# An unused buffer of 32 bytes ahead of the activation buffers of a two-block transformer kernel

## The chip, the cores and the metric

The kernel runs on one core of one Trainium2 chip. The metric is the device time in microseconds of one execution. TensorE (PE in the profile) multiplies, VectorE (DVE) and ScalarE (ACT) do the elementwise work, and SyncE (SP) issues the DMAs. SBUF, the on-chip memory, has 128 partitions; a buffer takes the same range of bytes in each of them, and "address" below means the byte in a partition where it starts.

## The reference

The reference runs 256 tokens of width 1024 through two blocks of two layers each, batch 1, float32.

```
def first_block(...):                                   # two layers
    h = rms_norm(x, norm_mix_g[l]); z = h @ w_in[l]
    y_rg = rg_lru(...) * gelu(a_y)                      # gated recurrence
    y_ml = mlstm_branch(...)                            # chunked matrix memory
    y_xa = memory_attention(xa_q, mem_n, w_kv[l])
    merged = g0 * (y_rg @ w_br_rg) + g1 * (y_ml @ w_br_ml) + g2 * (y_xa @ w_br_xa)
    x = x + merged @ w_out[l]
    x = x + (swiglu(h2, w1, w3, w2) if l == 0 else moe_swiglu(h2, ...))   # 8 experts, top 2
def second_block(...):                                  # two layers, tokens and 256 context tokens
    h_x = modulate(rmsnorm(x, ...), shift, scale)       # shift and scale from silu(c) @ ada_w
    o_x, o_c = mixer_ab(...) if layer == 0 else mixer_c(...)
    x = x + mod_x[2] * o_x; x = x + mod_x[5] * swiglu_2(h_x, w1, w3, w2)   # layer 0: ctx as well
```

All weights together are some 700 MB, and each is used once, on at most 512 tokens.

## The kernel before

**Precision and the general product.** Weights arrive in float32 as tiles of 128 x 2048 (1 MB; 8 blocks of 128 inputs by 256 outputs, for the experts' second product 2 blocks by 1024). A tile lands in RAW (three slots), in the expert stage in turn in RAW or in one of five of the F buffers. ACT copies it to WH in the format float32r (line 1899), and DVE subtracts that from the tile and writes the rest to WL (line 2299). Activations are kept as such pairs too: PH and PL (three pairs of 8 x 256), HPH and HPL (8 x 512), HDH and HDL (8 x 512), and YS with the experts' results. Each product is then three matmuls in float32r, in this order (lines 1566 to 1568):

```
T_.matmul(out, lh, rh, start=first, stop=False)
T_.matmul(out, lh, rl, start=False, stop=False)
last = T_.matmul(out, ll, rh, start=False, stop=end)
```

The second argument is the stationary operand (up to 128 columns are loaded into the array), the third the moving one (256 or 512 columns are streamed). In the trace a matmul is named PS<-moving,stationary.

**Forms.** In the rows form (most dense layers: the input projections, the branches, both feed-forward networks) the stationary operand is a slice of 128 columns of WH or WL, and the moving one a block of activations with 256 or 512 tokens. In the token form (values of the attentions, `tok` and `dtok`) it is the other way round: 128 tokens are stationary and 256 columns of WH or WL stream. The experts' first products (lines 1517 to 1519: stationary the gathered tokens in PH, PL or YS, moving WH or WL, 256 columns) and second products (lines 1835 to 1837: 512 columns of WH or WL against PH or PL) are like the token form. Line 1806 gathers an expert's tokens and lines 1846 and 1847 scatter its result back; both of their operands are activation buffers. Line 1699 to 1701 multiply the recurrence's gate weights, a tile with 36 columns.

**Order.** A planner writes one list of units by its own costs; each engine's program runs through that list. Engines wait for one another by semaphores. A tile's DMA waits until the tile that had the slot is split, WH and WL (three slots each) until the product that used them is done. The core runs first the first block (0 to some 1183 us its dense and attention parts, to some 2157 us the experts) and then the second.

**Placement.** `build` allocates the buffers one after another in one stack. Each takes its size, rounded up to a multiple of 32 bytes. `with ExitStack() as s1` opens a group whose buffers are freed at its end, so that the next ones lie over them: CAU, TMP1, F and P of the first block share their bytes with HP, BIAS, CST2, BAND, GN, TMP2, G, PQ and HD of the second, and YS (behind PAD) with F0 and F1. The last buffer ahead of all these is MOD.

Of the kernel before, what the change touches and what calls it, by code (L numbers as in the profile page):

```python
# [2919 lines left out]
def build(nc, io):  # L2920
    with ExitStack() as ctx:
        def sb(name, shape, dt=F32, stack=ctx):
            return stack.enter_context(nc.sbuf_tensor(name, shape, dt))
        mem = {}
        mem["RAW"] = sb("RAW", [128, NRAW, 2048])
        mem["WH"] = sb("WH", [128, NHL, 2048], F32R)
        mem["WL"] = sb("WL", [128, NHL, 2048], F32R)
        mem["X"] = sb("X", [128, 8, T])
        mem["CTX"] = sb("CTX", [128, 8, T])
        mem["PAR"] = sb("PAR", [128, NPAR])  # L2930
        mem["CST"] = sb("CST", [128, NCST])
        mem["SM"] = sb("SM", [128, 128])
        mem["RT"], mem["MK"], mem["GT"] = (mem["SM"][:, a:b] for a, b in ((0, 66), (66, 82), (82, 98)))
        mem["IDX"] = mem["SM"][:, 98:114].bitcast(U32)
        mem["LAMS"] = sb("LAMS", [128, 16])
        mem["ACOL"] = sb("ACOL", [128, 8])
        mem["R"] = sb("R", [128, 3, T])
        mem["LV"] = sb("LV", [128, 2])
        mem["LVS"] = sb("LVS", [128, 8])
        mem["POS"] = sb("POS", [128, 32])  # L2940
        mem["GC"] = sb("GC", [128, 3])
        mem["FLAG"] = sb("FLAG", [1, 1], mybir.dt.int32)
        mem["C32"] = sb("C32", [128, 262])
        mem["MROW"] = sb("MROW", [128, 512])
        mem["MOD"] = sb("MOD", [128, 2, 2, 48])
        mem["PS"] = ctx.enter_context(nc.psum_tensor("PS", [128, 8, 512], F32))
        with ExitStack() as s1:
            mem["CAU"] = sb("CAU", [128, 384], F32, s1)
            mem["TMP1"] = sb("TMP1", [128, 4, T], F32, s1)
            mem["F"] = [mem["CTX"] if i == 4 else sb(f"F{i}", [128, 8, T], F32, s1) for i in range(8)]  # L2950
            mem["P"] = [(sb(f"PH{i}", [128, 8, T], F32R, s1), sb(f"PL{i}", [128, 8, T], F32R, s1)) for i in range(3)]
        with ExitStack() as s2:
            sb("PAD", [128, 384 + 4 * T], F32, s2)
            mem["YS"] = sb("YS", [128, 16, T], F32R, s2)
        mem["HP"] = (sb("HPH", [128, 8, 512], F32R), sb("HPL", [128, 8, 512], F32R))
        mem["BIAS"] = sb("BIAS", [128, 512])
        mem["CST2"] = sb("CST2", [128, NCST2])
        mem["BAND"] = sb("BAND", [128, 640], F32R)
        mem["GN"] = sb("GN", [128, 2, 2, 2, 8])
        mem["TMP2"] = sb("TMP2", [128, 4, 512])  # L2960
        with ExitStack() as s3:
            mem["G"] = [sb(f"G{i}", [128, 4, 512], F32, s3)[:, :, :] for i in range(6)]
            mem["PQ"] = sb("PQ", [128, 3584], F32, s3)
            mem["LM"], mem["LAMB"] = mem["PQ"][:, 0:128], mem["PQ"][:, 128:384]
        with ExitStack() as s4:
            mem["HD"] = (sb("HDH", [128, 8, 512], F32R, s4), sb("HDL", [128, 8, 512], F32R, s4))
        v = views(mem)
        plan = Plan(io, mem, v)
        ledger = Ledger(lambda name: ctx.enter_context(nc.semaphore(name)))
        none = Nothing()  # L2970
        tensor_program(none, none, Engine(ledger, none, "pe", True), plan, mem, v)
        scalar_program(none, none, Engine(ledger, none, "act", True), plan, mem, v)
        vector_program(none, none, Engine(ledger, none, "dve", True), plan, mem, v)
        sync_program(none, none, Engine(ledger, none, "sp", True), plan, mem, v)
        block = ctx.enter_context(nc.Block())

        @block.sync
        def _(eng):
            sync_program(nc, nc.sync, Engine(ledger, eng, "sp", False), plan, mem, v)

        @block.tensor
        def _(eng):
            tensor_program(nc, nc.tensor, Engine(ledger, eng, "pe", False), plan, mem, v)

        @block.scalar
        def _(eng):
            scalar_program(nc, nc.scalar, Engine(ledger, eng, "act", False), plan, mem, v)

        @block.vector
        def _(eng):  # L2990
            vector_program(nc, nc.vector, Engine(ledger, eng, "dve", False), plan, mem, v)
# [104 lines left out]
```

How the kernel before makes its waits and increments, by code:

```python
    def wait_ge(self, what, *key):  # L90
        what = self.pre + what
        if self.counting:
            return
        n = self.ledger.value[(what,) + key]
        if self.seen.get(what, 0) < n:
            self.eng.wait_ge(self.ledger.sem(what), n)
            self.seen[what] = n
# [5 lines left out]
    def freed(self, key):  # L103
        if key is None or self.counting:
            return
        by = self.ledger.handed.get((self.pre,) + key)
        if by is not None:
            return self.wait_for(by)
        for what in ("free_a", "free_d"):
            if (self.pre + what,) + key in self.ledger.value:
                return self.wait_ge(what, *key)
        raise KeyError(key)
# [1 line left out]
    def wait_for(self, thing):  # L115
        n = self.ledger.value[thing]
        if self.seen.get(thing[0], 0) < n:
            self.eng.wait_ge(self.ledger.sem(thing[0]), n)
            self.seen[thing[0]] = n
# [1 line left out]
    def turn(self, made):  # L121
        made.then_inc(*self.done("turn_" + self.tag, self.steps))
        self.wait_ge("turn_" + self.tag, self.steps)
        self.steps += 1
# [1396 lines left out]
    def weight(key):  # L1522
        t = plan.tile[key]
        pe.wait_ge("w_hi", t.s)
        pe.wait_ge("w_lo", t.s)
        return t
# [1 line left out]
    def consts():  # L1528
        pe.wait_ge("par")
        pe.wait_ge("cst")
# [1 line left out]
    def lin(name, t, i, part, parts, side=None):  # L1532
# [27 lines left out]
        for j, (lh, ll, rh, rl) in enumerate(pairs):  # L1560
            if norm:
                pe.wait_ge("lo", norm, ks[j] // 2)
            if "each" in g.more:
```

## Time and profile before

| what | value |
|---|---|
| time, median of 3 runs | 3374.03 us (3371.98 to 3382.2) |
| span of the profiled execution | 3378.7 us |
| PE, weight loads, DVE, ACT busy | 96%, 88%, 69%, 54% |
| mean granted clock of TensorE | 0.976 |
| moved by DMA | 723.62 MB, mean 214 GB/s |

The profiled span is taken on the core from the first to the last instruction. Busy time of PE is the time in which at least one matmul is under way. Matmuls overlap (the next one starts while the last results of the one ahead drain), so PE's pace is read from the distance between starts in the timeline, and not from the length of one.

### The profile page before, as it was taken

What the parts mean: (1) busy time and instruction counts of PE and PEld (TensorE: products, weight loads), DVE (VectorE), ACT (ScalarE), POOL (GpSimd) and SP (SyncE); (2) the same over time, 40 slices, a digit from 0 to 9 for tenths busy, and PEclk for the clock granted to TensorE, in tenths of its full rate; (3) what the DMA queues carried; (4) which work ended last, traced back from release to release, by engine and by line L of the source; (5) the groups of instructions that cost most, each with busy time, mean ns of one, the idle gap of its engine ahead of it and who ended that gap; (6) DMA issues with size and microseconds to landing.
All of it is one profiled execution on the core that took longest, in us unless ns stands there. A gap on an engine that the chain in (4) does not pass through costs nothing.

```text
span 3378.7 us, 56020 instructions
## 1 busy us (share of the span) xinstructions
PE 3229.4 (96%) x24147; PEld 2988.9 (88%) x24147; DVE 2334.0 (69%) x2984; ACT 1831.6 (54%) x2188; POOL 0.2 (0%) x4
## 2 busy tenths in 40 slices
PE   8999999999899899999999999899899999999898
PEld 7998999999889799999999999778687989985698
DVE  6877655577776688888888888755575565556455
ACT  5564544455644477777777777633454444334443
POOL 0000000000000000000000000000000000000000
PEclk9999999999999899999999999999899999998899
DMA  6433565454335699899899899621333466530353
GB/s 255 164 138 125 187 236 193 158 193 159 125 125 188 269 367 363 331 357 357 331 356 356 338 357 354 249 85 63 113 136 127 141 234 251 199 124 13 145 187 118
DMA packets 102812, 723.62 MB, mean 214 GB/s; under 512 B 11424, under 2 KB 13344, under 8 KB 16672
## 3 DMA queue, kind: packets, MB, share of 16 engines
q1 hardware_dynamic: 102560, 719.97, 57.3%
q8 instruction: 194, 3.18, 0.4%
q14 instruction: 58, 0.48, 0.0%
HBM read 718.87 MB, written 1.05 MB: 213 GB/s over the span
## 4 chain that ended last, share of the span: by engine, by line
PE 80%; DVE 10%; ACT 7%; issue 2%; DMA 1%; SPq 0%; DVEq 0%; ACTq 0%
PE PS L1566 14%; PE PS L1568 13%; PE PS L1567 13%; PE PS L1517 6%; PE PS L1519 6%; PE PS L1518 6%; DVE WL L2299 4%; PE PS L1835 3%; PE PS L1836 3%; PE PS L1837 3%; ACT WH L1899 3%; PE PS L1677 2%; PE PS L1648 2%; PE PS L1621 1%; PE PS L1665 1%
## 5 line engine op out<-in xcount | busy, mean ns | idle before, releaser
L2299 DVE TENSOR_TENSOR WL<-RAW,WH 128x2048 fp32r<-128x2048 f32 (+2 forms) x428 | 962.8, 2252 | 548.3 <-ACT WH L1899 543.2
L1899 ACT ACTIVATE WH<-RAW 128x2048 fp32r<-128x2048 f32 (+2 forms) x428 | 803.4, 1880 | 243.1 <-PE PS L1568 182.6
L1566 PE MATMUL PS<-PH,WH 128*128 128x256 f32 x2464 | 705.5, 286 | 22.6 <-ACT F L1981 6.1
L1567 PE MATMUL PS<-PL,WH 128*128 128x256 f32 x2464 | 696.4, 283 | 0.0
L1568 PE MATMUL PS<-PH,WL 128*128 128x256 f32 x2464 | 696.3, 283 | 0.0
L2299 DVE TENSOR_TENSOR WL<-F,WH 128x2048 fp32r<-128x2048 f32 x210 | 480.8, 2290 | 79.8 <-ACT WH L1899 79.1
L1566 PE MATMUL PS<-HPH,WH 128*128 128x256 f32 (+1 forms) x1648 | 493.2, 299 | 17.8 <-ACT WH L1899 8.7
L1566 PEld LDWEIGHTS PS<-PH,WH 128*128 128x128 f32 x2464 | 468.9, 190 | 29.2 <-issue 20.5
L1567 PE MATMUL PS<-HPL,WH 128*128 128x256 f32 (+1 forms) x1648 | 481.2, 292 | 0.0
L1568 PE MATMUL PS<-HPH,WL 128*128 128x256 f32 (+1 forms) x1648 | 480.6, 292 | 0.0
L1567 PEld LDWEIGHTS PS<-PL,WH 128*128 128x128 f32 x2464 | 469.1, 190 | 0.6
L1568 PEld LDWEIGHTS PS<-PH,WL 128*128 128x128 f32 x2464 | 468.7, 190 | 0.0
L1899 ACT ACTIVATE WH<-F 128x2048 fp32r<-128x2048 f32 x210 | 403.7, 1923 | 72.1 <-PE PS L1837 48.2
L1517 PE MATMUL PS<-WH,PH 128*128 128x256 f32 x1456 | 417.4, 287 | 2.0 <-DVE WL L2299 1.1
L1518 PE MATMUL PS<-WL,PH 128*128 128x256 f32 x1456 | 407.4, 280 | 0.0
L1519 PE MATMUL PS<-WH,PL 128*128 128x256 f32 x1344 | 376.9, 280 | 0.0
L1566 PEld LDWEIGHTS PS<-HPH,WH 128*128 128x128 f32 x1648 | 317.7, 193 | 36.4 <-issue 20.3
L1567 PEld LDWEIGHTS PS<-HPL,WH 128*128 128x128 f32 x1648 | 318.1, 193 | 4.3
L1568 PEld LDWEIGHTS PS<-HPH,WL 128*128 128x128 f32 x1648 | 317.7, 193 | 4.5
L1517 PEld LDWEIGHTS PS<-WH,PH 128*128 128x128 f32 x1456 | 275.2, 189 | 5.4 <-ACT WH L1899 1.2
L1518 PEld LDWEIGHTS PS<-WL,PH 128*128 128x128 f32 x1456 | 275.6, 189 | 2.8
L1519 PEld LDWEIGHTS PS<-WH,PL 128*128 128x128 f32 x1344 | 253.9, 189 | 0.0
(394 smaller groups left out, 4972.1 us busy)
## 6 DMA issues: line engine op xcount, KB each, us to landing
F<-in_moe_w SPq DMA_DIRECT2D x210, 1024.0 KB, 5.6
RAW<-in_ffn_w SPq DMA_DIRECT2D x130, 1024.0 KB, 5.0
RAW<-in_moe_w SPq DMA_DIRECT2D x126, 1024.0 KB, 5.2
RAW<-in_w_in SPq DMA_DIRECT2D x64, 1024.0 KB, 5.0
F<-in_ada_w SPq DMA_DIRECT2D x18, 1024.0 KB, 11.3
RAW<-in_w_kv SPq DMA_DIRECT2D x16, 1024.0 KB, 5.0
G<-in_ada_w SPq DMA_DIRECT2D x15, 1024.0 KB, 9.0
RAW<-in_w_in_ab SPq DMA_DIRECT2D x12, 1024.0 KB, 5.0
```

Of the source, the lines that this page charges most:

```text
L1517: T_.matmul(out, lh, rh, start=i == 0, stop=False)
L1518: T_.matmul(out, lh, rl, start=False, stop=False)
L1519: last = T_.matmul(out, ll, rh, start=False, stop=i == n - 1)
L1566: T_.matmul(out, lh, rh, start=first, stop=False)
L1567: T_.matmul(out, lh, rl, start=False, stop=False)
L1568: last = T_.matmul(out, ll, rh, start=False, stop=end)
L1648: last = T_.matmul(ps, l, r, start=i == 0, stop=i == len(ops) - 1 and not spec["bias"])
L1835: T_.matmul(out, oh[:, c], wh, start=j == 0 and k == 0, stop=False)
L1836: T_.matmul(out, oh[:, c], wl, start=False, stop=False)
L1837: last = T_.matmul(out, ol[:, c], wh, start=False, stop=j == 13 and k == 1)
L1899: S.activation(mem["WH"][:, t.s % NHL, 0:m], v.raws[t.slot][:, 0:m], ACT.Copy).then_inc(*ac.done("w_hi", t.s))
L2299: V.tensor_tensor(mem["WL"][:, t.s % NHL, 0:m], v.raws[t.slot][:, 0:m], mem["WH"][:, t.s % NHL, 0:m].bitcast(F32), sub).then_inc(*dv.done( ...
```

## The change

One line is added to `build`, behind the last of the buffers that live through the whole kernel. It allocates a buffer EDGE of 8 float32 values (32 bytes) in each partition, which nothing reads or writes.

```
--- before.py
+++ after.py
@@ -2944,6 +2944,7 @@
         mem["MROW"] = sb("MROW", [128, 512])
         mem["MOD"] = sb("MOD", [128, 2, 2, 48])
         mem["PS"] = ctx.enter_context(nc.psum_tensor("PS", [128, 8, 512], F32))
+        sb("EDGE", [128, 8])
         with ExitStack() as s1:
             mem["CAU"] = sb("CAU", [128, 384], F32, s1)
             mem["TMP1"] = sb("TMP1", [128, 4, T], F32, s1)
```

The instructions, their order, their waits and the DMAs are the same on every engine. What moves is the address of every buffer that is allocated behind EDGE, by 32 bytes (addresses of the built programs):

| buffer | address before | modulo 64 | address after | modulo 64 |
|---|---|---|---|---|
| RAW, WH, WL | 16512, 41088, 65664 | 0 | the same | 0 |
| X, CTX | 90240, 98432 | 0 | the same | 0 |
| MOD | 116320 | 32 | the same | 32 |
| CAU and HPH | 117088 | 32 | 117120 | 0 |
| F0 and YS | 122720 | 32 | 122752 | 0 |
| HPL | 133472 | 32 | 133504 | 0 |
| TMP2 | 157280 | 32 | 157312 | 0 |
| G0 and HDH | 165472 | 32 | 165504 | 0 |
| PH0, PL0 | 180064, 188256 | 32 | 180096, 188288 | 0 |
| PQ | 214624 | 32 | 214656 | 0 |

The buffers between them (F1 to F7, PH1 to PL2, G1 to G5, HDL, BIAS, CST2, BAND, GN, TMP1) are 32 modulo 64 before and 0 after in the same way. Rows inside the buffers are multiples of 512 or 1024 bytes apart, so the blocks that the products read start like their buffer; after the change they have the same address modulo 128 as the blocks of WH and WL. Small buffers that stay where they are (SM, LAMS, ACOL, LVS, MROW, MOD) keep their 32 modulo 64.

## Rows read from the trace of the kernel before

**Rows 1.** The page: span, busy time of each engine, granted clock in 40 slices.
```profile
span 3378.7 us, 56020 instructions
...
PE 3229.4 (96%) x24147; PEld 2988.9 (88%) x24147; DVE 2334.0 (69%) x2984; ACT 1831.6 (54%) x2188; POOL 0.2 (0%) x4
```

**Rows 2.** Stretches: us, then busy us of PE, PEld, DVE, ACT, POOL; clock, DMA share.
```profile
124.50:146.00 21.50, 21.50 (x187) 21.50 (x186) 20.78 (x21) 7.69 (x5) 0.00 (x0) 1.00 0.53 192
340.00:680.00 340.00, 336.11 (x2865) 332.24 (x2864) 195.87 (x229) 155.74 (x168) 0.00 (x0) 1.00 0.54 195
1183.00:2157.00 974.00, 973.77 (x6963) 910.03 (x6962) 841.40 (x609) 705.16 (x612) 0.00 (x0) 1.00 0.93 349
```

**Rows 3.** The page's chain that ended last, by engine and by line.
```profile
PE 80%; DVE 10%; ACT 7%; issue 2%; DMA 1%; SPq 0%; DVEq 0%; ACTq 0%
PE PS L1566 14%; PE PS L1568 13%; PE PS L1567 13%; PE PS L1517 6%; PE PS L1519 6%; PE PS L1518 6%; DVE WL L2299 4%; PE PS L1835 3%; PE PS L1836 3%; PE PS L1837 3%; ACT WH L1899 3%; PE PS L1677 2%; PE PS L1648 2%; PE PS L1621 1%; PE PS L1665 1%
```

**Rows 4.** PE's groups by shape: label moving,stationary; busy us, mean ns, idle before.
```profile
L1566 PE MATMUL PS<-PH,WH 128*128 128x256 f32 x2464 | 705.5, 286 | 22.6 <-ACT F L1981 6.1 <-DVE PL L2390 5.6 <-issue 4.3
...
L1566 PE MATMUL PS<-HPH,WH 128*128 128x256 f32 x1552 | 452.3, 291 | 13.5 <-DVE HPL L2393 7.2 <-ACT WH L1899 4.3 <-ACT G L2053 0.8
...
L1517 PE MATMUL PS<-WH,PH 128*128 128x256 f32 x1456 | 417.4, 287 | 2.0 <-DVE WL L2299 1.1 <-ACT PL L2172 1.0
...
L1566 PE MATMUL PS<-HDH,WH 128*128 128x256 f32 x352 | 99.2, 282 | 0.0
...
L1566 PE MATMUL PS<-WH,PH 128*128 128x256 f32 x160 | 44.7, 279 | 0.0
...
L1566 PE MATMUL PS<-HPH,WH 128*128 128x512 f32 x96 | 40.9, 426 | 4.4 <-ACT WH L1899 4.4
```

**Rows 5.** PE in order of time, feed-forward: first and last of 195 matmuls.
```profile
519.84 0.28 PE L1566 MATMUL PS<-PH,WH 128*128 128x256 f32 x1
...
542.79 0.28 PE L1568 MATMUL PS<-PH,WL 128*128 128x256 f32 x1
```

**Rows 6.** PE in order of time, token form of the keys and values: 192 matmuls.
```profile
124.05 0.28 PE L1566 MATMUL PS<-WH,PH 128*128 128x256 f32 x1
...
146.33 0.28 PE L1568 MATMUL PS<-WH,PL 128*128 128x256 f32 x1
```

**Rows 7.** PE in order of time, 512 columns, projection stage: 23 matmuls.
```profile
2299.17 0.39 PE L1567 MATMUL PS<-HPL,WH 128*128 128x512 f32 x1
...
2304.30 0.40 PE L1568 MATMUL PS<-HPH,WL 128*128 128x512 f32 x1
```

**Rows 8.** PE in order of time, 512 columns, an expert's second product: 12 matmuls.
```profile
1356.49 0.39 PE L1835 MATMUL PS<-WH,PH 128*128 128x512 f32 x1
...
1359.05 0.40 PE L1837 MATMUL PS<-WH,PL 128*128 128x512 f32 x1
```

**Rows 9.** PE in order of time, an expert's scatter back: 16 matmuls.
```profile
1305.58 0.28 PE L1846 MATMUL PS<-PL,YS 128*128 128x256 f32 x1
...
1307.37 0.28 PE L1847 MATMUL PS<-PL,YS 128*128 128x256 f32 x1
```

**Rows 10.** PE in order of time, gate weights of 36 columns: 24 matmuls.
```profile
169.16 0.28 PE L1699 MATMUL PS<-PH,WH 128*36 128x256 f32 x1
...
169.85 0.28 PE L1699 MATMUL PS<-PH,WH 128*36 128x256 f32 x1
...
171.86 0.28 PE L1701 MATMUL PS<-PH,WL 128*36 128x256 f32 x1
```

**Rows 11.** Splits of a weight tile, by source: ACT's copy and DVE's subtraction.
```profile
L1899 ACT ACTIVATE WH<-RAW 128x2048 fp32r<-128x2048 f32 x409 | 780.3, 1911 | 214.9 <-PE PS L1568 154.5 <-PE PS L1837 29.6 <-PE PS L1519 14.3
...
L1899 ACT ACTIVATE WH<-F 128x2048 fp32r<-128x2048 f32 x210 | 403.7, 1923 | 72.1 <-PE PS L1837 48.2 <-PE PS L1519 23.9
```

**Rows 12.** The page's DMA issues: KB each, median us from issue to landing.
```profile
F<-in_moe_w SPq DMA_DIRECT2D x210, 1024.0 KB, 5.6
...
RAW<-in_moe_w SPq DMA_DIRECT2D x126, 1024.0 KB, 5.2
```

More of the change, by code:

```diff
@@ L2946, in build @@
         mem["PS"] = ctx.enter_context(nc.psum_tensor("PS", [128, 8, 512], F32))
+        sb("EDGE", [128, 8])
         with ExitStack() as s1:
```

## The prediction

> **What bounds the kernel now.** I read the page's busy times first. TensorE (PE) is busy 3229.4 of 3378.7 us, DVE 2334.0 and ACT 1831.6 [rows 1]. The stretches show where that holds: in the feed-forward stage from 340 to 680 us PE is busy 336.1 of 340 us, and in the expert stage from 1183 to 2157 us 973.8 of 974 us [rows 2]. So nearly everywhere the time is the number of matmuls times the step from one matmul's start to the next one's. The mean length of a matmul in the groups (280 to 290 ns) is not that step, since matmuls overlap; the step has to be read from the timeline. The chain that ended last agrees: PE has 80% of it, and lines 1566, 1567 and 1568 (the general product) 40% of the span [rows 3].
>
> The change moves no instruction. It moves the start of every buffer behind it by 32 bytes, so the question is which engine's work depends on where in 64 bytes an operand starts. The raw tiles RAW, the split tiles WH and WL, X and CTX start at multiples of 64 in both kernels. All of F, P (PH, PL), HP, HD, YS, G, PQ, TMP start at 32 past one before, and at 0 after. I call the two places 32 and 0. In the trace's names the first operand of a matmul is the moving one (it streams 256 or 512 columns), the second the stationary one (128 columns of weights). Four combinations of moving and stationary places exist, and the kernel before has three of them:
>
> Moving at 32, stationary at 0 (the rows form, activations stream against split weights): in the feed-forward stage 195 matmuls start from 519.84 to 542.79 us, 194 steps, 22.95 us, **118.3 ns** a step [rows 5].
>
> Moving at 0, stationary at 32 (the token form and the experts' up products, split weights stream against activations): 192 matmuls from 124.05 to 146.33 us, 191 steps, **116.65 ns** [rows 6]. Both stretches have the granted clock at 1.00, the 2.4 GHz level [rows 2]. It is the same line 1566 and the same 256 columns, and the groups show the same difference in the length of one: 282 ns for PS<-HDH,WH and 279 ns for PS<-WH,PH, both without any idle time before them [rows 4].
>
> Both at 32 (an expert's scatter back): 16 matmuls from 1305.58 to 1307.37 us, 15 steps, **119.3 ns** [rows 9].
>
> Both at 0 is what the change makes of all of them, and no row shows it. That is the open price here.
>
> **The change part by part.** The unused buffer itself costs no instruction. Its worth is in these parts.
>
> The rows form with 256 columns. Its groups count 2464, 1552 and 352 on each of three lines [rows 4], 13,104 matmuls; the output projection of the last attention (lines 1582 to 1584) adds 192 by the code. Bounds for its step after the change: from above 119.3 ns, the nearest row in which both operands have the same place [rows 9]; from below 115.0 ns, the lowest step of a stretch with 256 columns, the first six steps from 169.16 to 169.85 us of the product with only 36 weight columns [rows 10] (over all its 23 steps, to 171.86 us, it is 117.4). I take 116.65, because it is the row with an aligned moving operand and the same 128 weight columns [rows 6], and because 512 columns take 233.2 ns a step (22 steps from 2299.17 to 2304.30 us) with the moving operand at 32 [rows 7] and 232.7 ns (11 steps from 1356.49 to 1359.05 us) with it at 0 [rows 8], twice 116.6. A step in proportion to the columns looks like the stream's own pace, on which 118.3 stands 1.65 ns. The gain is 13,296 x 1.65 ns = 21.9 us.
>
> The scatter back and the gather of the experts, both at 32 before, 128 matmuls each by the code: 2.7 ns off each of 256, 0.7 us.
>
> The experts' up products and the token form, 3 x (1456 + 336) and 480 matmuls, only the stationary operand moves from 32 to 0: bounds 115.6 to 119.3 ns, taken as no change (116.65), by the same stream pace. The 512-column products likewise: rows 7 and 8 differ by half a nanosecond although opposite operands are at 32.
>
> Sum on PE: 22.6 us. How much reaches the end? Lines 1566 to 1568 hold some 1673 us of steps (13,104 x 118.3 ns, 480 x 116.65 ns, 288 x 233.2 ns), and the chain gives them 40% of 3378.7, 1351 us, or 81% [rows 3]; so at least 18.3 us. Where PE is busy without a gap [rows 2] all of it counts. I take 21 us. What is late next there: nothing, since in the feed-forward stage DVE is busy 195.9 and ACT 155.7 of 340 us and the DMA share is 0.54 [rows 2].
>
> ACT and DVE. ACT's split copy takes 1911 ns from RAW (at 0) and 1923 ns from F (at 32), 210 of these [rows 11]: 2.5 us of ACT time, hidden, because PE stands still 0.2 us in the whole expert stage [rows 2]. If that cover were gone it would be worth at most 2.5 us.
>
> DMA. Expert tiles that go to F land 5.6 us after issue, those to RAW 5.2 us [rows 12]. If that 0.4 us is the place of the destination it goes away, and again PE has no wait in that stage that it could shorten: nothing. That stage moves 349 GB/s at a DMA share of 0.93 [rows 2], so it could not run much faster either.
>
> The Trainium skill speaks against all this: its page "Advanced Engine Details and Errata", section Memory Cachelines, gives SBUF lines of 16 bytes, full speed for accesses that stay in one. Both 0 and 32 are starts of such a line, so by that rule the sum would be nothing, against the 22.6 us above. The trace has a step that differs by 1.65 ns between two placements [rows 5, 6], which the rule alone doesn't explain.
>
> **The profiled execution and the median.** The profiled span is 3378.7 us, the median of the three runs 3374.0 us, 4.7 us below it. A difference of 21 us is the same on either. Predicted: 3374 - 21 = 3353 us.
>
> **The rivals.**
>
> *The two costs add up.* From the three rows, the stationary place costs 119.3 - 118.3 = 1.0 ns and the moving one 119.3 - 116.65 = 2.65 ns; both at 0 would be 115.65 ns. The rows form gains 13,104 x 2.65 = 35 us, the others 5,856 x 1.0 = 6 us, scatter and gather 1 us: 42 us, 3332 us. For it: the narrow product reaches 115.0 ns [rows 10]. Against it: 512 columns take twice 116.6 ns [rows 7, 8]. With all at 115.0 ns it would be 53 us, 3321 us, the far end. A still lower step (106.7 ns is 256 columns at 2.4 GHz) has no row near it.
>
> *Slower: the operands get in each other's way when they start at the same place.* PE reads the stationary columns of the next matmul while the present one streams. The only matmuls before with both operands at one place have the longest step, 119.3 ns [rows 9]; the mixed ones have 118.3 and 116.65 [rows 5, 6]. If the cause is equal places and not the place 32, the change puts every product there: 13,104 x 1.0 + 5,856 x 2.65 = 13 + 16 = 29 us more, 3403 us. It decides from a step of 117.8 ns upward: there what the rows form wins and what the others lose cancel. Against it: in both mixed cases the distance is 32 modulo 64, yet they differ by 1.65 ns, so the moving operand's own place must count for something.
>
> *Nothing.* The 1.65 ns belongs to the form and not to the place: in the rows form the stationary operand is a slice of half a row of a split tile and the moving one a whole row of activations. Then the step stays at 118.3 ns, gain 0, 3374 us. This is also what the skill's line of 16 bytes would give. Against it: 512 columns in the rows form show no extra [rows 7].
>
> **How the numbers follow.** The forecast (3349 to 3358 us) has a chance of 0.48, adding up 0.17, nothing 0.17, equal places 0.18. A measurement of this kernel can tell about 0.3% (10 us) from no change; so faster 0.65, same 0.17, slower 0.18. The range leaves out only the slower case: from 3321 us less 3 us of spread to 3374 us plus 6 us (the runs before lie within 10 us), 3318 to 3380 us.
>
> **What would show it.** In the profile after, the feed-forward stretch that took 22.95 us for 194 steps takes 22.6 us; length of PS<-HDH,WH falls from 282 to 279 ns; the token form keeps 116.65 ns and the 512-column products 233 ns; scatter back falls from 119.3 to some 116.7 ns; the expert stage keeps its 974 us. If the scatter back keeps 119.3 ns and the expert stage grows by some 15 us, equal places are the cause. If both forms fall to 115.7 ns, the costs add up. If the rows form keeps 118.3 ns, the place is not the cause. The forecast is wrong too if a stage's time moves while its matmul step does not.

## The result and the profile after: slower by 0.7%, because moving and stationary operands now start at equal places

The changed kernel takes 3397.19 us (median of four runs, 3396.51 to 3401.66), the kernel before beside it 3373.01 us (median of four, 3367.34 to 3382.2). The ratio is 1.0069, interval 1.0054 to 1.0084: 24.2 us slower. The prediction was 3353 us, 3318 to 3380 us. Both its sign and its range were wrong; the case it had as the slower rival (3403 us, with a chance of 0.18) is the one that happened.

The page of the profiled execution after: span and busy times, the chain by engine, and the issues of the experts' tiles.

```profile
span 3394.7 us, 56020 instructions
...
PE 3254.8 (96%) x24147; PEld 3022.7 (89%) x24147; DVE 2337.2 (69%) x2984; ACT 1829.2 (54%) x2188; POOL 0.2 (0%) x4
...
PE 79%; DVE 11%; ACT 6%; issue 2%; DMA 2%; SPq 0%; DVEq 0%; ACTq 0%
...
F<-in_moe_w SPq DMA_DIRECT2D x210, 1024.0 KB, 5.6
...
RAW<-in_moe_w SPq DMA_DIRECT2D x126, 1024.0 KB, 5.4
```

PE's busy time rose by 25.4 us against [rows 1], the span by 16.0 us; all other engines kept theirs. F's tiles still land 5.6 us after issue although F now starts at a multiple of 64 [rows 12]: the destination's place was not what they lost against RAW.

The groups of PE and ACT by shape, after (busy us, mean ns of one, idle before):

```profile
L1566 PE MATMUL PS<-PH,WH 128*128 128x256 f32 x2464 | 709.5, 288 | 20.3 <-ACT F L1981 5.9 <-DVE PL L2390 4.8 <-issue 4.1
...
L1517 PE MATMUL PS<-WH,PH 128*128 128x256 f32 x1456 | 420.9, 289 | 2.1 <-ACT PL L2172 1.1 <-DVE WL L2299 1.0
...
L1566 PE MATMUL PS<-HDH,WH 128*128 128x256 f32 x352 | 99.9, 284 | 0.0
...
L1899 ACT ACTIVATE WH<-F 128x2048 fp32r<-128x2048 f32 x210 | 402.3, 1917 | 74.1 <-PE PS L1837 45.4 <-PE PS L1519 28.7
```

Each of the three PE groups grew by about 2 ns a matmul (from 286, 287 and 282 ns in [rows 4] to 288, 289 and 284), with about the same idle time ahead of them. The exact steps are in PE's timeline after. In order: the rows form in the feed-forward stage (195 matmuls, as in [rows 5]); the token form (192, as in [rows 6]); 512 columns in the projection stage (23, as in [rows 7]); an expert's second product (12, as in [rows 8], of a later expert); a scatter back (16, as in [rows 9], of a later expert).

```profile
519.68 0.28 PE L1566 MATMUL PS<-PH,WH 128*128 128x256 f32 x1
...
542.96 0.28 PE L1568 MATMUL PS<-PH,WL 128*128 128x256 f32 x1
...
124.20 0.28 PE L1566 MATMUL PS<-WH,PH 128*128 128x256 f32 x1
...
147.12 0.28 PE L1568 MATMUL PS<-WH,PL 128*128 128x256 f32 x1
...
2283.57 0.40 PE L1567 MATMUL PS<-HPL,WH 128*128 128x512 f32 x1
...
2288.60 0.39 PE L1568 MATMUL PS<-HPH,WL 128*128 128x512 f32 x1
...
2152.51 0.40 PE L1835 MATMUL PS<-WH,PH 128*128 128x512 f32 x1
...
2155.03 0.39 PE L1837 MATMUL PS<-WH,PL 128*128 128x512 f32 x1
...
1825.22 0.28 PE L1846 MATMUL PS<-PL,YS 128*128 128x256 f32 x1
...
1827.01 0.28 PE L1847 MATMUL PS<-PL,YS 128*128 128x256 f32 x1
```

Last less first, by the number of steps: 23.28 us by 194 is **120.0 ns** (before 118.3), 22.92 by 191 is **120.0 ns** (before 116.65), 5.03 by 22 is **228.6 ns** (before 233.2), 2.52 by 11 is **229.1 ns** (before 232.7), and the scatter back keeps 119.3 ns. The timeline gives times to 0.01 us, so over 15 steps a value is sure only to 0.7 ns, over 11 steps to 0.9 ns, and over 190 steps to 0.05 ns. So both forms with 256 columns now have one step, higher than either had, and the 512-column products have become faster.

What that makes over the whole kernel follows from the means of all gapless stretches of the two traces. The rows form with 256 columns has 118.32 ns before and 119.92 after, the token form 116.68 and 119.92, the experts' first product 116.92 and 119.65, 512 columns 233.20 and 229.13 with experts, 233.28 and 228.70 without. 13,296 x 1.60 + 960 x 3.24 + 5,376 x 2.73 - 1,344 x 4.07 - 288 x 4.58 is 21.3 + 3.1 + 14.7 - 5.5 - 1.3 = 32 us. Measured are 24.2 us.

The stage in which PE hardly waits (busy 1010.18 of 1015.70 us before) shows the sum best. Below are the stretches up to the first expert, the experts, and the rest, first of the kernel before, then after (columns: busy us of PE, PEld, DVE, ACT, POOL; granted clock, DMA share, GB/s):

```profile
0.00:1160.30 1160.30, 1094.40 (x8784) 1058.19 (x8784) 787.66 (x1132) 580.21 (x742) 0.20 (x4) 0.98 0.49 177
1160.30:2176.00 1015.70, 1010.18 (x7219) 943.55 (x7220) 872.24 (x634) 733.00 (x636) 0.00 (x0) 1.00 0.91 343
2176.00:3378.70 1202.70, 1124.83 (x8147) 987.18 (x8145) 674.11 (x1219) 518.38 (x812) 0.00 (x0) 0.96 0.38 141
```

```profile
0.00:1168.70 1168.70, 1110.77 (x8783) 1073.26 (x8784) 788.35 (x1132) 579.47 (x742) 0.20 (x4) 0.98 0.49 176
1168.70:2193.30 1024.60, 1019.43 (x7220) 959.68 (x7220) 873.77 (x634) 732.79 (x636) 0.00 (x0) 1.00 0.91 340
2193.30:3394.70 1201.40, 1124.57 (x8146) 989.74 (x8145) 675.05 (x1219) 516.91 (x811) 0.00 (x0) 0.97 0.39 141
```

The expert stage grew by 8.9 us, with the clock at 1.00 in both; its terms of the sum give 14.7 - 5.5 = 9.2 us. The first part grew by 8.4 us. The last part did not grow in these two executions, but its granted clock was 0.97 after and 0.96 before. Of a span of 3378.7 us at a mean of 0.976 some 160 us are at the lower level (1.2 GHz), of 3394.7 us at 0.979 some 142 us. The profiled executions therefore differ by 16.0 us while the medians differ by 24.2 us, and the comparisons below go by medians.

### The profile page after: what moved, and what is told of

Its sections match the earlier page's. It is cut to its first block, busy times and chain, and to the rows that moved or that the text cites. A ratio compares the mean times of both kernels' runs of the same rounds, so it can differ in the third digit from the quotient of the medians.

```text
span 3394.7 us, 56020 instructions
## 1 busy us (share of the span) xinstructions
PE 3254.8 (96%) x24147; PEld 3022.7 (89%) x24147; DVE 2337.2 (69%) x2984; ACT 1829.2 (54%) x2188; POOL 0.2 (0%) x4
## 4 chain that ended last, share of the span: by engine, by line
PE 79%; DVE 11%; ACT 6%; issue 2%; DMA 2%; SPq 0%; DVEq 0%; ACTq 0%
PE PS L1566 14%; PE PS L1567 13%; PE PS L1568 13%; PE PS L1517 6%; PE PS L1518 6%; PE PS L1519 6%; DVE WL L2299 4%; PE PS L1835 3%; PE PS L1836 3%; PE PS L1837 3%; ACT WH L1899 3%; PE PS L1677 2%; PE PS L1648 2%; PE PS L1621 1%; PE PS L1665 1%
## 5 line engine op out<-in xcount | busy, mean ns | idle before, releaser
L1566 PEld LDWEIGHTS PS<-PH,WH 128*128 128x128 f32 x2464 | 476.3, 193 | 27.0 <-issue 20.4
L1567 PEld LDWEIGHTS PS<-PL,WH 128*128 128x128 f32 x2464 | 476.6, 193 | 0.7
L1568 PEld LDWEIGHTS PS<-PH,WL 128*128 128x128 f32 x2464 | 476.3, 193 | 0.0
L1899 ACT ACTIVATE WH<-F 128x2048 fp32r<-128x2048 f32 x210 | 402.3, 1917 | 74.1 <-PE PS L1837 45.4
```

What stands on the lines that cost most here:

```text
L1899: S.activation(mem["WH"][:, t.s % NHL, 0:m], v.raws[t.slot][:, 0:m], ACT.Copy).then_inc(*ac.done("w_hi", t.s))
```

## The experiments

Two theories stood after the result. **Equal places**: the step depends on how far the stationary operand starts from the moving one, over some period, and distance 0 is costly. **Own places**: it depends on where each operand lies by itself, and 0 modulo 64 (or 128) happens to be a bad one. Distance below is the start of the stationary operand less that of the moving one, modulo 256. WH and WL start at 128 modulo 256, the activation buffers at 96 before and 128 after. So before, the rows form has +32 and the token form -32; after, both have 0. "The map" is the table of steps that the first small kernel gives.

### place_map: all starts of 0 to 112 bytes against each other

A kernel of PE alone. For 256 and for 512 columns, groups of 48 matmuls (order and buffers as in the general product) step through 8 x 8 starts of the two operands.

```
for st, mv, j in ((0, 0, 0), (0, 1, 1), (1, 0, 2)):
    S_, M_ = (wh, wl)[st], (ph, pl)[mv]
    last = T_.matmul(out_, S_[:, s + 256 * k:s + 256 * k + 128], M_[:, m + n * k:m + n * k + n], ...)
```

> This kernel leaves the whole computation out: it loads x, copies it into four float32r buffers that start at multiples of 128 bytes, and runs only matmuls, in the kernel's own order of three per block, once for each pair of starts of the moving and the stationary operand, 0 to 112 bytes past a multiple of 128 in steps of 16, with 256 columns (48 matmuls a pair) and then with 512. Theory 'equal places' (the two operands that PE reads at once get in each other's way when their starts are equal modulo 64): with 256 columns the step is 120.0 ns on the pairs with a distance of 0 or 64, and 116.7 to 118.3 ns where it is 32 or 96, whatever the moving operand's own start. Theory 'absolute start' (a start at 0 modulo 64 is slow in itself for 256 columns): the step goes by the row or the column of the map, not by the distance, and 32 against 32 stays under 0 against 0. Either way 32 against 32 must show the 119.3 ns of the scatter back, 0 against 0 the 120.0 ns of the changed kernel, and 512 columns 229 ns at 0 against 0 and 233 ns at 96 against 0. Other multiples of 16: the narrow product's 115 ns suggests that some distance is under 116.7 ns.

PE's timeline of that kernel, first and last of 48 matmuls with 256 columns, in five groups. Moving and stationary start are 0 and 0, 0 and 32, 0 and 64, 32 and 0, 32 and 32.

```profile
32.54 0.28 PE L59 MATMUL PS<-PH,WH 128*128 128x256 f32 x1
...
38.18 0.28 PE L59 MATMUL PS<-PH,WL 128*128 128x256 f32 x1
...
43.98 0.28 PE L59 MATMUL PS<-PH,WH 128*128 128x256 f32 x1
...
49.54 0.28 PE L59 MATMUL PS<-PH,WL 128*128 128x256 f32 x1
...
55.31 0.28 PE L59 MATMUL PS<-PH,WH 128*128 128x256 f32 x1
...
60.64 0.28 PE L59 MATMUL PS<-PH,WL 128*128 128x256 f32 x1
...
123.09 0.28 PE L59 MATMUL PS<-PH,WH 128*128 128x256 f32 x1
...
128.57 0.28 PE L59 MATMUL PS<-PH,WL 128*128 128x256 f32 x1
...
134.45 0.28 PE L59 MATMUL PS<-PH,WH 128*128 128x256 f32 x1
...
140.08 0.28 PE L59 MATMUL PS<-PH,WL 128*128 128x256 f32 x1
```

Over 47 steps: 120.0, 118.3, 113.4, 116.6 and 119.8 ns. The first, second and fourth are the three steps of the two kernels, out of a kernel that has nothing else in it. Both operands at 32 cost what both at 0 cost, so own places fall. Equal places modulo 64, as the expectation had them, fall too: a distance of 64 was to have 120.0 ns and has 113.4, so the period is longer than 64. The table (ns a step, 256 columns, from the trace) shows the same of all starts that are multiples of 32: moving the pair along by 32 keeps the value.

| moving start | stationary 0 | 32 | 64 | 96 |
|---|---|---|---|---|
| 0 | 120.0 | 118.4 | 113.3 | 118.8 |
| 32 | 116.7 | 119.9 | 118.4 | 113.3 |
| 64 | 117.8 | 116.6 | 119.9 | 118.4 |
| 96 | 120.0 | 117.8 | 116.7 | 120.0 |

With 512 columns equal starts are the fast case: 226.7 ns at 0 and 0, 233.4 at 0 and 32, 233.3 at 32 and 0. That is the gain of the long products after the change. Where both start at an odd multiple of 16 the pattern is another one (16 and 16 has 116.7, 16 and 80 has 113.3 ns), so the distance alone can be the rule only for multiples of 32. The 226.7 ns of the small kernel are not reached by the changed kernel, which has 229.1 ns at the same distance; why was not looked into.

### edge_64, edge_96 and second_only: other distances in the whole kernel

```
-        sb("EDGE", [128, 8])
+        sb("EDGE", [128, 16])        # edge_64; edge_96: [128, 24]
```

edge_64 puts the activations at 160, the same place modulo 64 as before but on the other side of WH; edge_96 puts them at 192. second_only leaves the first block as before and has the unused buffer ahead of HP, so that only the second block gets distance 0:

```
         with ExitStack() as s2:
             sb("PAD", [128, 384 + 4 * T], F32, s2)
             mem["YS"] = sb("YS", [128, 16, T], F32R, s2)
+        sb("EDGE", [128, 8])
         mem["HP"] = (sb("HPH", [128, 8, 512], F32R), sb("HPL", [128, 8, 512], F32R))
```

> The unused buffer has 64 bytes in place of 32, so the activations start at 32 modulo 128 (before: 96, after the change: 0). If only the distance modulo 64 counts, all steps are those of before (118.3 ns rows, 116.7 ns token form and experts) and the time is 3373 us. If the distance modulo 128 counts, with its sign, rows and token form change roles: rows 116.7 ns (13,296 x -1.65 = -22 us), token form and experts 118.3 ns (6336 x +1.65 = +10 us), 3361 us. Theory 'absolute start' expects the times of before as well.

> The unused buffer has 96 bytes, the activations start at 64 modulo 128. If only the place modulo 64 counts, by either theory, this is the changed kernel again: 120.0 ns for all products with 256 columns, 229 ns for 512, 3397 us. If the distance modulo 128 counts, 64 is a distance that no kernel so far has, and the step may be anything from 115 to 120 ns.

> The unused buffer of 32 bytes stands behind the groups of the first block, ahead of HP: only the second block's buffers move. If the added time is the step of the matmuls and nothing else, the first block keeps its 118.3 and 116.7 ns, and the second takes 120.0 ns: 5904 x 1.7 + 480 x 3.3 - 288 x 4.5 ns = 10 us more, 3383 us, and the expert stage is unchanged. If the loss sits in the expert stage or in something that a single shift of all buffers brings, this kernel is near 3373 us.

edge_64, PE's timeline: first and last of 195 matmuls of the rows form, then of 192 of the token form.

```profile
519.70 0.28 PE L1566 MATMUL PS<-PH,WH 128*128 128x256 f32 x1
...
542.33 0.28 PE L1568 MATMUL PS<-PH,WL 128*128 128x256 f32 x1
...
123.75 0.28 PE L1566 MATMUL PS<-WH,PH 128*128 128x256 f32 x1
...
146.36 0.28 PE L1568 MATMUL PS<-WH,PL 128*128 128x256 f32 x1
```

116.6 and 118.4 ns: the two forms have changed roles against [rows 5, 6], as distances of -32 and +32 would have it. This alone refutes the step on which the prediction rested, that an operand at 0 modulo 64 is the faster moving operand: here the moving one is at 32 modulo 64 and has 116.6 ns. Time: 3369.80 us against 3373.49, ratio 0.9990 (0.9978 to 1.0002). The steps came as expected, the 3361 us that were worked out from them did not: the interval includes no change at all, so this run shows its point by the steps and not by the time.

edge_96, distance -64 in the rows form and +64 in the token form; 192 matmuls of the token form:

```profile
123.91 0.28 PE L1566 MATMUL PS<-WH,PH 128*128 128x256 f32 x1
...
145.57 0.28 PE L1568 MATMUL PS<-WH,PL 128*128 128x256 f32 x1
```

113.4 ns. Most of the rows form ran at 117.8 ns, some of its stretches at 113.3 (mean 117.3). Time: 3358.61 us against 3373.49, ratio 0.9956 (0.9939 to 0.9972). All buffers of the products start at multiples of 64 here, as in the changed kernel, and yet it is 38.6 us faster than that one: being at a multiple of 64 is not what costs.

second_only, second block, 195 matmuls of the rows form:

```profile
3201.14 0.28 PE L1567 MATMUL PS<-HPL,WH 128*128 128x256 f32 x1
...
3224.41 0.28 PE L1566 MATMUL PS<-HPH,WH 128*128 128x256 f32 x1
```

119.9 ns, while the first block kept 118.3. Its time is 3382.89 us against 3373.49, ratio 1.0023 (1.0013 to 1.0033), 9.4 us more where 10 were expected. So a part of the loss goes with a part of the placement, and the other buffers that the change moved (F, which DVE, ACT and the DMAs use) are not needed for it.

### w_plus_32 and distance_map: the other operand, and the period

w_plus_32 leaves the activations at 96 and moves WH and WL to 160: the small buffer ACOL is allocated ahead of them (X and CTX, behind them, move along). Distances are +64 (rows) and -64 (token). distance_map is place_map with stationary starts up to 496 and some moving starts up to 256, and two kinds of groups in which the starts alternate by 64 bytes: in "next" the stationary operand of the next matmul always lies 64 bytes past the moving one (a matmul's own at 128 and 0 in turn), in "own" it is the other way round.

```
         mem["RAW"] = sb("RAW", [128, NRAW, 2048])
+        mem["ACOL"] = sb("ACOL", [128, 8])
         mem["WH"] = sb("WH", [128, NHL, 2048], F32R)
...
-        mem["ACOL"] = sb("ACOL", [128, 8])
```

> The 32-byte buffer ACOL is allocated ahead of WH and not behind SM, with no new buffer: WH, WL, X, CTX move by 32 bytes and all the activations stay where they were before. From activations to weights the distance is now +64. Theory 'distance': rows form 113.3 ns (13,296 x -5.0 ns = -66 us on TensorE), token form and experts at the opposite distance 117.8 ns (6336 x +1.1 ns = +7 us), 512 columns within a nanosecond or two; some 3318 us if all of it arrives, 3325 us if a tenth is lost to waits. Theory that a start at 0 or 32 modulo 64 counts for itself: rows would be both at 32, 119.3 ns as in the scatter back, and the time about 3390 to 3400 us.

> The computation is left out again; only matmuls on four buffers with the same start modulo 256, 48 per pair of starts. Scanned is the distance from the moving operand's start to the stationary one's over 0 to 496 bytes in steps of 16, with 256 and 512 columns, then the moving operand's own start over 64, 128, 192 and 256. Theory 'distance' (the map of the first run went along its diagonals): the step is a function of the distance modulo 256, the second half of each scan repeats the first, and the moving operand's own start at a multiple of 32 changes nothing: 120.0 ns at 0, 113.3 at +64, 118.4 at +32, 117.8 at 192 (that is -64), 116.7 at 224 (that is -32). Theory 'own start' would have other values at +64 once the moving operand starts at 64 or 192. Last, the starts alternate between 0 and 64 from one matmul to the next: if the conflict is between the streaming operand and the weights that are read meanwhile for the next matmul, the variant whose next weights always lie 64 bytes on gives 113.3 ns and the one whose own weights do gives the mean of distances 0 and 128; if it is between the two operands of one matmul, it is the other way round.

w_plus_32 took 3352.87 us against 3374.94, ratio 0.9934 (0.9918 to 0.9951). Moving the weights by 32 works like moving the activations by 32 the other way: neither form shows the 119.3 ns that the theory of own places wanted for the rows form. But the time is some 28 us above even the 3325 us expected: the rows form did not have 113.3 ns everywhere. PE's timeline shows a thing that the map had not: one form, one distance, two steps. Below are 195 matmuls of the rows form at 519 us and 195 at 3173 us.

```profile
519.68 0.28 PE L1567 MATMUL PS<-PL,WH 128*128 128x256 f32 x1
...
542.53 0.28 PE L1566 MATMUL PS<-PH,WH 128*128 128x256 f32 x1
...
3173.82 0.28 PE L1566 MATMUL PS<-HPH,WH 128*128 128x256 f32 x1
...
3195.81 0.28 PE L1568 MATMUL PS<-HPH,WL 128*128 128x256 f32 x1
```

117.8 and 113.35 ns. The first belongs to a stretch of 1463 matmuls at 117.78 ns throughout, the second to one of 1473 at 113.33 ns throughout. Within these stretches the step doesn't wander; it is taken up at the start and kept.

distance_map: the value repeats every 256 bytes (all stationary starts 0 to 240 and 256 to 496 agree, for moving starts 0 and 16). Against moving 0, distance 128 has 118.8 ns, 160 has 119.8, 192 has 113.3, 224 has 116.7; at moving starts of 64, 128, 192 and 256 distance 0 has 119.9 to 120.0, 64 and 192 have 117.8. Two of the values expected by distance are therefore not met: 192 against moving 0 was to have 117.8 ns, and 64 was to have 113.3 ns at the other moving starts. These are the two steps of w_plus_32 again. With 512 columns 0 has 226.7, 192 has 228.8 and most others 232 to 234. The alternating groups have 117.7 to 117.9 ns (next) and 118.7 to 118.8 (own). The first could be the higher of the two steps of distance 64, which would speak for the stream and the next weights, but the second is not the 119.4 ns in the middle of distances 0 and 128 that this would want; so they don't tell which reads meet.

### two_paces: one placement, started at different times

Groups of 24 matmuls, each behind a lone matmul of 32 to 200 columns that shifts it in time.

```
if gap:
    T_.matmul(out_[:, 0:gap], wh[:, 0:128], ph[:, 0:gap], start=True, stop=True)
```

> The computation is left out; only matmuls. At a distance of 64 bytes the two kernels edge_96 and w_plus_32 held a step of either 113.3 or 117.8 ns through a whole run of up to 1463 matmuls, and changed it only where PE had stood still. Here each distance is taken several times with 24 matmuls of 256 columns, each group behind a lone matmul of another number of columns, which shifts the group in time. Theory 'locked paces': at 64 and 192 bytes the groups split into some of 113.3 and some of 117.8 ns by the columns of the lone matmul; at 0 all keep 120.0 ns, at 224 all 116.7 ns, at 32 all 118.3 ns. Theory 'place alone' (the step is fixed by the starts, and the whole kernels differ for another reason, the DMA or the other engines): all groups of one distance agree. The distances between multiples of 16 bytes are taken to see whether one has 113.3 ns always.

Distance 0 had 120.0 or 119.6 ns in all of its groups, 32 had 118.5 in all eight, 48 and 192 had 117.8, 128 had 118.7. Distance 64 had 113.3, 117.7, 113.3, 113.3, 117.8, 113.3, 117.8, 113.3. PE's timeline, the second to the last matmul of its first two groups, with a lone matmul of 32 and of 56 columns ahead:

```profile
121.74 0.28 PE L66 MATMUL PS<-PL,WH 128*128 128x256 f32 x1
...
124.24 0.28 PE L66 MATMUL PS<-PH,WL 128*128 128x256 f32 x1
...
124.58 0.28 PE L66 MATMUL PS<-PL,WH 128*128 128x256 f32 x1
...
127.17 0.28 PE L66 MATMUL PS<-PH,WL 128*128 128x256 f32 x1
```

22 steps take 2.50 us (113.6 ns) and 2.59 us (117.7 ns), of the same operands in the same order. So at 64 the step depends on when the stretch starts, at 0 and 32 it doesn't. It does at -32 (224) as well, against the expectation: five groups had 116.7 to 116.9 ns and three 117.7 to 117.8. Of the starts at odd multiples of 16, 16 with 16 had 116.7, 120.0, 118.2 and 118.3, while 16 with 80 had 113.3 ns in all four of its groups.

### who_meets_whom and shift_16: the width of the operands, and a version by the map

who_meets_whom varies what place_map keeps: 8, 32, 64 or 128 weight columns, 128 or 384 moving columns, alternating starts once more, and four pairs of starts at distance 64. shift_16 is the whole kernel with WH and WL at 208 modulo 256, P, HP and HD at 144 and YS at 128. 208 against 144 is 16 + 64 against 16, moved along by 128.

```
-        mem["WH"] = sb("WH", [128, NHL, 2048], F32R)
-        mem["WL"] = sb("WL", [128, NHL, 2048], F32R)
+        mem["LAMS"] = sb("LAMS", [128, 16])
+        def parts(name, at, n, shape, pad, stack=ctx):
+            size = shape[0] * shape[1]
+            whole = sb(name, [128, n * size + pad], F32R, stack)
+            return [whole[:, at + i * size:at + (i + 1) * size].rearrange("p (a n) -> p a n", a=shape[0]) for i in range(n)]
+        mem["WH"], mem["WL"] = parts("W", 4, 2, (NHL, 2048), 8)
...
-        mem["HP"] = (sb("HPH", [128, 8, 512], F32R), sb("HPL", [128, 8, 512], F32R))
+        mem["HP"] = tuple(parts("HP", 4, 2, (8, 512), 8))
```

> The computation is left out; only matmuls, each group of 24 behind a lone matmul of another number of columns. Three questions. First, do the weights take part? Groups with 128, 64, 32 and 8 weight columns at distances 0, 32, 64, 128, 192 and 224 bytes. Theory 'two readers' (the stream of the moving operand and the read of the next weights meet in the same memory): with 8 columns the step is short and hardly depends on the distance. Theory 'start of the stream' (only the moving operand's place or the instruction itself costs): the same steps as with 128 columns. Second, which two meet? The starts alternate by 32 bytes, once so that the weights of the next matmul always lie at the place of the stream (next equal), once so that those of the matmul itself do (own equal): 'two readers' gives 120.0 ns for the first and 116.7 to 118.5 ns for the second, and the opposite would show that a matmul's own two operands meet. Third, 128 and 384 columns, and the pairs of starts (16, 80), (80, 16), (144, 208), (208, 144) bytes, with eight groups each: if a step of 113.3 ns does not hang on the moment at those starts, all eight show it.

> P, HP and HD start at 144 and WH and WL at 208 modulo 256, by 16 bytes of padding ahead of each (F, G and the other buffers keep multiples of 32; YS keeps 128). In the maps these two starts had 113.3 ns both ways round, in every group. If that holds in the whole kernel: rows form 13,296 x -5.0 = -66 us, token form and experts without YS 5328 x -3.4 = -18 us, experts with YS 1008 x up to +3.3 = +3 us, together -81 us, 3292 us, or 3300 us if the expert stage meets the limit of the DMA (its tiles would have to come at 371 GB/s). If the places of 16 bytes cost ACT or DVE, or the paces of the full kernel lock otherwise than in the map, no better than w_plus_32, 3350 us.

With only 8 weight columns the distance counts for almost nothing: 32, 64, 128, 192 and 224 give the same four values, 116.6, 113.3, 113.3 and 116.7 ns for the four lone matmuls, and 0 gives 115.5 to 116.7. PE's timeline, 16 matmuls at distance 224 (15 steps, 113.3 ns):

```profile
294.82 0.28 PE L68 MATMUL PS<-PH,WL 128*8 128x256 f32 x1
...
296.52 0.28 PE L68 MATMUL PS<-PH,WL 128*8 128x256 f32 x1
```

So the width of the weights decides whether the distance counts, which speaks for their loading as the other party. It is not shown by itself, since fewer weight columns also mean fewer rows of results written. 64 and 32 weight columns still have an effect of the distance, with other values (0 gives 113.3 to 120.0 with 64 columns). With 128 moving columns every distance has 111.5 to 112.0 ns, with 384 columns all have 173.1 to 174.7 except 128 with 176.0. Alternating starts gave 118.2 to 118.6 ns (next equal) and 118.5 to 119.1 (own equal), where the theory of the next weights wanted 120.0 for the first and at most 118.5 for the second: again no answer. Of the pairs at distance 64, 16 with 80 and 144 with 208 had 113.3 ns in all eight groups; the opposite ones did not: 208 with 144 had 118.3 in all eight, 80 with 16 both 118.3 and 113.3. A stationary start of 76 against 0, no multiple of 16, had 113.3 to 113.7 ns in all eight groups here and in its three of two_paces; no whole kernel has tried it.

shift_16 shows both signs. Its page, and 195 matmuls of the rows form:

```profile
span 3326.3 us, 56020 instructions
...
PE 3168.0 (95%) x24147; PEld 2933.4 (88%) x24147; DVE 2332.6 (70%) x2984; ACT 1830.6 (55%) x2188; POOL 0.2 (0%) x4
```

```profile
519.68 0.28 PE L1567 MATMUL PS<-P,W 128*128 128x256 f32 x1
...
541.66 0.28 PE L1566 MATMUL PS<-P,W 128*128 128x256 f32 x1
```

The rows form has 113.3 ns here and 113.6 as a mean over the kernel. The token form, in which the roles are exchanged (208 with 144), has 118.4, worse than before; the experts' first product has 116.9 on average, as before; their second 227.5. The expectation had 113.3 ns for the token form and the experts too, and 3292 to 3300 us: it rested on the small kernels having 113.3 ns both ways round, which who_meets_whom refutes for 208 with 144. Time: **3328.63 us** against 3372.66, ratio 0.9864 (0.9848 to 0.9881). It is the fastest version of this study, 44.0 us below the kernel before and 68.6 us below the changed one, with the same instructions.

### What the steps explain of the times

For each kernel of the whole computation the steps of its own trace are summed as above and set beside the difference of the medians.

| kernel | distance, rows / token | rows, token, experts' first: ns | 512 columns, experts: ns | sum of steps | measured |
|---|---|---|---|---|---|
| before | +32 / -32 | 118.3, 116.7, 116.9 | 233.2 | | |
| after | 0 / 0 | 119.9, 119.9, 119.7 | 229.1 | +32 us | +24.2 us |
| edge_64 | -32 / +32 | 116.8, 118.3, 118.5 | 233.2 | -10 us | -3.7 us |
| edge_96 | -64 / +64 | 117.3, 114.7, 114.9 | 233.0 | -27 us | -14.9 us |
| second_only | +32 / -32, second block 0 / 0 | 119.0, 118.2, 116.9 | 233.3 | +9.5 us | +9.4 us |
| w_plus_32 | +64 / -64 | 116.1, 115.9, 117.8 | 229.5 | -30 us | -22.1 us |
| shift_16 | +64 / -64, from 16 | 113.6, 118.4, 116.9 | 227.5 | -70 us | -44.0 us |

The order is right in every row. second_only meets its sum; in the others the time is less than the sum, by a quarter to two thirds. Part of the remainder can be seen. PE stands idle 149.3 us before (span less busy, [rows 1]), 139.9 us after, and 158.3 us in shift_16: a faster PE waits longer where other engines are last, a slower one less. And shift_16 has a mean granted clock of 0.974, some 173 us at the lower level against some 160 before. The clock takes a part of the gain from every faster kernel: over the runs of each, the mean granted clock is 0.978 before and after, 0.9764 in edge_64, 0.9755 in edge_96, 0.9768 in w_plus_32 and 0.9752 in shift_16. Over the 19 runs of the kernel before beside edge_64, the time falls by 1.8 us with each 0.001 of clock. By that (an estimate) the clock cost edge_64 some 2.5 us, edge_96 4, w_plus_32 2.3 and shift_16 5.6 us. In the expert stage, where neither idle time nor clock differs, shift_16 gains 7.3 us (1015.7 to 1008.4 us) against 7.7 us by the steps. What is left is not settled.

## Why the prediction was wrong

**The bound was right.** PE's step sets the time: the chain gives PE 79% after and 80% before, and the time goes the way of the steps in every kernel.

**The step that failed is the price of "both at 0".** The prediction took 116.65 ns for the rows form, from the token form, because that row had "an aligned moving operand". It had also a stationary operand 32 bytes below, and this was the cause. Each row that was at hand had two properties, the place of each operand and the distance between them, and the three rows could be read by either. The row with distance 0 was there: the scatter back, 119.3 ns [rows 9], which the prediction took as the upper bound of the forecast and as the price of its slower rival. It was the true value within 0.7 ns, since the map gives 119.9 to 120.0 for any pair at distance 0 whose starts are multiples of 32. The term of the rows form, put at 21.9 us gained (13,296 x 1.65 ns), was 21.3 us lost: the feed-forward stretch that was to take 22.6 us took 23.28.

**The reason against the slower rival was wrong.** It was set aside because +32 and -32 are the same distance modulo 64 and yet differ by 1.65 ns. The period is 256, as distance_map shows, so the two are different distances; edge_64 exchanges them. A difference that a theory "can't explain" only counts against it if its period is known, and no row gave that.

**"The stream's own pace" was wrong.** 233.2 ns for 512 columns looked like twice 116.6, and from that the token form and the experts' products were taken to be at a floor. Neither was: 512 columns went to 228.6 ns and can go to 226.7, and 256 columns went up to 120.0 and can go to 113.3. The two are not in proportion, and their best distances differ. These terms, all put at nothing, are token form and experts' first product +18 us and 512 columns -7 us. The sign had already turned with the rows form; they add 11 us to its 21.3.

**A count was wrong.** The token form was counted as 480 matmuls; the trace has 160 on each of three lines with PH and as many with HPH, 960. The rival's 5,856 should have been 6,336, which makes its 29 us 30. With them the steps on lines 1566 to 1568 are 1729 us and not 1673, and the chain's 1351 us are 78% of them, so that the 18.3 us were no firm lower end. Neither matters for the outcome.

**The rival was right in kind, and close in part by luck.** Its 3403 us against 3397.19 come of errors that cancel: the products with 256 columns lost 39 us by their steps and not 29, the 512-column products gave back 7, and 24.2 of the remaining 32 us arrived. The range, 3318 to 3380 us, left this case out although it had a chance of 0.18.

**What was right.** ACT's copies from F went from 1923 to 1917 ns and changed nothing; the experts' tiles in F kept their 5.6 us from issue to landing (RAW's went from 5.2 to 5.4); the scatter back kept 119.3 ns, which the prediction had named as the sign of equal places, and the expert stage grew by 8.9 us where that sign spoke of 15: its first products lost 14.7 us and the 512-column products gave 5.5 back.

The Trainium skill, page "Advanced Engine Details and Errata", section Memory Cachelines, gives SBUF lines of 16 bytes and full speed for accesses within one. As the prediction read it, a shift by two whole lines would change nothing; measured were 24.2 us, and steps from 113.3 to 120.0 ns between placements that all start at a line, and the measurement decides. The section says nothing of two operands read at the same time.

## What to carry to other kernels

Where matmuls follow one another without a gap, the start of the moving operand relative to the stationary one can be worth several per cent of PE's step. Make the distance between them, modulo 256 bytes, a thing that is measured with the kernel's own shapes in a small kernel of PE alone: putting all buffers at multiples of 64 bytes gave the slowest step for 256 columns where it made the starts equal (the changed kernel) and 113.3 or 117.8 ns where it left 64 bytes between them (edge_96). And before a price is taken from a neighbouring row, write down every property in which that row differs from the case wanted; here the nearest row by one property was the farthest by the one that counted.

## What the runs showed of the hardware that was not expected

- Float32r matmuls with 256 moving and 128 weight columns, starts at multiples of 32: distance 0 has 120.0 ns, +32 has 118.4, 128 has 118.7, in groups shifted in time as well (119.6 to 120.0, 118.5, 118.7). -32 has 116.7, but 117.7 to 117.8 in three of eight shifted groups. The value repeats with 256 bytes.
- At distance 64 or 192 a stretch takes up one of two steps, 113.3 or 117.8 ns, and keeps it for over a thousand matmuls. At 64 it was shown to go by when the stretch starts; at 192 both steps were seen, but not in the groups shifted in time, which all had 117.8. At 16 with 80 and at 144 with 208 it was always 113.3 ns.
- 512 columns: 226.7 ns at distance 0, 228.8 at 192, 232 to 234 at most others. 384 columns: 173.3 ns, 128 columns: 111.7 ns, nearly independent of it (384 has 176.0 at 128); so are 256 columns against only 8 weight columns.
- Which reads meet, the stream's and the load of the next weights or of the matmul's own, and why the step locks in, was tried with alternating starts and stays open.
- The place of a DMA's destination at 32 modulo 64 was worth nothing (5.6 us to landing before and after), that of ACT's source 6 ns of 1923.
- The faster kernels were granted a little less clock (0.9752 in shift_16, 0.978 before, means over their runs). Why is open.
